# A two-layer hybrid encoder kernel: the second layer's output projection in seven block products, in one function with the gate

## What is computed

```python
# x: (1536, 1024), layer 1 (odd)
h = rmsnorm(x, g_pre)
z = h @ w_in                      # latents, gate g_c, FNet input f_in, gate g_d
c_out = mla_attention(...) * silu(g_c)        # 8 heads of 64 columns: 512 columns
d_out = fft2(f_in).real * silu(g_d)           # 512 columns
o = concat([c_out, d_out]) @ w_out            # output projection, 1024 x 1024
x = x + rmsnorm(o, g_post)                    # called x1 below
x = x + sigmoid(x @ w_ple_gate) * (p @ w_ple) # gate, 1024 x 1024, and embedding, 256 x 1024
```

## Time and profile before

| what | value |
|---|---|
| median of 3 runs | 1996.87 us (1994.7 to 2001.17) |
| the profiled execution | 1996.65 us, of which the span is 1994.9 |
| PE busy | 1921.7 us (96%), 9784 matmuls and transposes |
| DVE busy | 1143.9 us (57%) |
| ACT busy | 687.1 us (34%) |
| POOL busy | 761.8 us (38%) |
| DMA, share of 16 engines | 43.0% |
| mean granted PE clock | 0.987 of full speed |

### The profile page before, as it was taken

How to read it: one execution, slowest core, us unless ns; L and a number is a source line. 1 busy time by engine, 2 the same in 40 slices (tenths; PEclk the granted TensorE clock), 3 DMA queues, 4 the chain that set the end, 5 groups by cost and what they waited for, 6 DMA issues and landing times. The chain is left out here.

```text
span 1994.9 us, 26356 instructions
## 1 busy us (share of the span) xinstructions
PE 1921.7 (96%) x9784; PEld 1603.8 (80%) x9784; DVE 1143.9 (57%) x1735; ACT 687.1 (34%) x1409; POOL 761.8 (38%) x538
## 2 busy tenths in 40 slices
PE   4999999999989999999989999999999999999999
PEld 3888888887889788788877888877898998788787
DVE  5599999826768317524754100175777776234775
ACT  6111212211578332212223111122677775323322
POOL 0111121122587544454533222133699851531101
PEclk8999999999999999999989999999999999999999
DMA  4202333443476556534320222286546332656734
GB/s 171 64 11 69 133 95 109 144 141 114 164 260 219 182 165 223 198 114 135 131 66 15 79 90 69 88 326 182 165 133 201 121 105 64 229 209 225 259 126 145
DMA packets 152242, 286.11 MB, mean 143 GB/s; under 512 B 31489, under 2 KB 70145, under 8 KB 152130
## 3 DMA queue, kind: packets, MB, share of 16 engines
q1 hardware_dynamic: 152130, 284.62, 43.0%
HBM read 181.61 MB, written 102.96 MB: 143 GB/s over the span
## 5 line engine op out<-in xcount | busy, mean ns | idle before, releaser
L593 DVE SCALAR_TENSOR_TENSOR ie_acc<-ie_u,ie_wconv,ie_acc 128x1551 f32<-128x1551 f32 x120 | 249.8, 2081 | 3.2
L191 POOL TENSOR_TENSOR w_lo_part<-w_raw,w_hi_part 128x1024 fp32r<-128x1024 f32 x24 | 66.3, 2763 | 335.0 <-ACT w_hi_part L183 335.0
L1598 PE MATMUL op_ps<-w_hi_part,rows_hi 128*128 128x512 f32 x384 | 157.1, 409 | 5.0 <-DVE rows_lo L1157 2.6
L173 POOL TENSOR_TENSOR w_hi_part<-w_raw,zero 128x1024 fp32r<-128x1024 f32 x48 | 92.8, 1933 | 173.7 <-DMA w_raw<-wall 171.9
L328 PE MATMUL ie_ps<-rows_hi,w_hi_part 128*128 128x512 f32 x384 | 153.1, 399 | 4.8 <-DVE w_lo_part L557 4.8
L1598 PE MATMUL op_ps<-w_hi_part,rows_lo 128*128 128x512 f32 x384 | 152.3, 397 | 0.0
L328 PE MATMUL ie_ps<-rows_hi,w_lo_part 128*128 128x512 f32 x384 | 152.1, 396 | 0.0
L1598 PE MATMUL op_ps<-w_lo_part,rows_hi 128*128 128x512 f32 x384 | 152.1, 396 | 0.0
L328 PE MATMUL ie_ps<-rows_lo,w_hi_part 128*128 128x512 f32 x384 | 151.1, 394 | 0.0
L2870 DVE TENSOR_TENSOR mla_pt_lo<-mla_ps_t,mla_pt_hi 128x512 fp32r<-128x512 f32 x160 | 108.9, 686 | 26.2 <-ACT mla_pt_hi L2839 25.1
L175 POOL TENSOR_TENSOR w_lo_part<-w_raw,w_hi_part 128x1024 fp32r<-128x1024 f32 x48 | 119.1, 2480 | 3.8
(11 more groups left out here) (291 smaller groups left out, 5088.6 us busy)
## 6 DMA issues: line engine op xcount, KB each, us to landing
w_raw<-wall SPq DMA_DIRECT2D x76, 512.0 KB, 4.6
op_in<-x SPq DMA_DIRECT2D x24, 512.0 KB, 4.5
x<-op_in SPq DMA_DIRECT2D x24, 512.0 KB, 3.0
weight_blocks<-w_hi_part SPq DMA_DIRECT2D x20, 512.0 KB, 4.9
w_hi_part<-weight_blocks SPq DMA_DIRECT2D x14, 512.0 KB, 6.8
w_lo_part<-weight_blocks SPq DMA_DIRECT2D x14, 512.0 KB, 6.7
pro_x<-x SPq DMA_DIRECT2D x12, 512.0 KB, 7.9
op_in<-attn SPq DMA_DIRECT2D x24, 256.0 KB, 3.1
```

Of the source, the lines that this page charges most:

```text
L173: pool.tensor_tensor(hi, raw, g.zero[:, 0:1].broadcast_to([P, QCOLS]), ALU.add).then_inc(g.w_hi, 1)
L593: dve.scalar_tensor_tensor(acc[:], ubuf[:, cc, s:s + CW], wconv[:, cc, s:s + 1], acc[:], ALU.mult, ALU.add).then_inc(taps, 1)
L1598: mm = pe.matmul(product_at(c * NT + t), g.XT[a][:, k, t * P:(t + 1) * P], w_at(g, name, m, k * HALF, HALF), start=k + a + m == 0, stop=k ...
```

## The change

The gate's block scheme is used for the output projection too, and both run in one function, `out_and_gate`, over 84 units: 42 for the projection and 42 for the gate, each a product of 12 matmuls.

- `out_proj` is no longer called for layer 1, nor `gate_blocks`; the attention output stays in SBUF (`g.attn_rows`) and the half products too (`u`, `v`, `o11` in place of `o_half` in DRAM).
- The weights of both are summed, split and stored in blocks: 28 pieces in place of 14. 7 pieces each follow prep of heads 2, 3, 5 and 6; the sums of the gate's blocks (8 additions) follow prep of head 4. Their raw blocks are loaded by SP after the 14 pieces of the projection are stored.
- The high part of a piece is now made by ACT inside its attention stream (`wb.high`, after the exponential of steps 12h-2 to 12h+4), POOL makes the low part alone (`wb.low`). `wb.high` of piece p waits until the high part of piece p-2 is stored and its low part is made. ACT's attention stream is written out in place of the loop.
- The ring of split rows is 6 long and filled 5 ahead. The first 5 are filled in the last steps of the attention.
- x1 of a tile is made at the units of `X1_STEP`, by four DVE operations of 512 columns, and PE turns it right after the next unit.

```diff
 def mla(g, ml, bl, wb):
...
-        CHUNKS = {2: range(4), 3: range(4, 8), 4: range(8, 11), 5: range(11, 14)}
+        CHUNKS = {2: range(7), 3: range(7, 14), 5: range(14, 21), 6: range(21, 28)}
+        W_HIGH = {NT * h - 2 + i: p for h, c in CHUNKS.items() for i, p in enumerate(c)}
...
         def _(sp):
...
-            wb.load_raw(sp)
+            wb.load_raw(sp, 0)
             for h in range(2, HEADS):
                 sp.wait_ge(ml.prepped, h * ml.PREPS)
                 ml.load(g, sp, h, slice(h * DH, (h + 1) * DH))
-                for i in CHUNKS.get(h - 1, []):
-                    wb.store(sp, i)
-                if h % 2:
-                    pl.wait(sp, "normed", (h - 1) * NG)
-                    store(slice((h - 3) * DH, (h - 1) * DH))
+                for p in CHUNKS.get(h - 1, []):
+                    wb.store(sp, p)
+                if h == 4:
+                    wb.load_raw(sp, 1)
             wb.wait_stored(sp)
...
         def _(pool):
             for h in range(1, HEADS):
                 pl.wait(pool, "weighed", (h - 1) * NG)
                 ml.prep(g, pool, h, h % 2)
-                if h == 1:
-                    wb.sum(pool)
-                for i in CHUNKS.get(h, []):
-                    wb.split(pool, i)
-            for n in quarters("out1_a"):
-                split_quarter(g, pool, n)
+                if h in (1, 4):
+                    wb.sum(pool, h // 4)
+                for p in CHUNKS.get(h, []):
+                    wb.low(pool, p)
...
+            for step in range(LAST + DRAIN):
+                if 0 <= step - 2 < LAST:
+                    hi(0, step - 2)
+                if step % 2 and 0 <= step - 5 < LAST:
+                    act_copy(act, 0, (step - 5) // 2)
+                if step < LAST:
+                    exp(0, step)
+                if step in W_HIGH:
+                    wb.high(act, W_HIGH[step])
+                if step == LAST + 4:
+                    act.wait_ge(ml.prepped, HEADS * ml.PREPS)
+                    for N in range(AHEAD):
+                        bl.high(act, N)
...
+    def high(self, act, p):
+        m, b, q, name = self.piece(p)
+        act.wait_ge(self.summed, 8 * (m + 1))
+        if p >= 2:
+            act.wait_ge(self.hi_stored[p % 2], 16 * (p // 2))
+            act.wait_ge(self.lo, p - 1)
+        act.copy(self.stage(p), self.area(name, q)).then_inc(self.hi, 1)
+
+    def low(self, pool, p):
+        m, b, q, name = self.piece(p)
+        pool.wait_ge(self.hi, p + 1)
+        pool.tensor_tensor(self.area(name, q, True), self.area(name, q), self.stage(p).bitcast(F32), ALU.subtract).then_inc(self.lo, 1)
...
+RING, AHEAD = 6, 5
+X1_STEP = [33, 34, 36, 37, 39, 40, 42, 43, 44, 45, 46, 47]
...
+def out_and_gate(g, bl, wb):
...
+            def x1_row(t):
...
+                dve.scalar_tensor_tensor(left, left, r, wide(bl.gpost[:, 0:HALF]), ALU.mult, ALU.mult).then_inc(x1_rows, 1)
+                dve.scalar_tensor_tensor(right, right, r, wide(bl.gpost[:, HALF:D]), ALU.mult, ALU.mult).then_inc(x1_rows, 1)
...
+                dve.tensor_tensor(wide(x[:, 0:HALF]), wide(x[:, 0:HALF]), left, ALU.add).then_inc(x1_rows, 1)
...
+                dve.tensor_tensor(wide(x[:, HALF:D]), wide(x[:, HALF:D]), right, ALU.add).then_inc(x1_rows, 1)
...
+            for N in range(N_ALL):
+                product(N)
+                if 0 <= N - 4 < NT:
+                    turn_main(N - 4)
+                if N - 1 in x1_at:
+                    turn_x1(x1_at[N - 1])
+                if N in of_unit:
+                    embedding(of_unit[N])
...
-            rows = OutRows(g, 1)
-            mla(g, ml, rows)
-            ple = Ple(g, 1)
-            out_proj(g, 1, rows, ple)
-            gate_blocks(g, ple)
+            bl, wb = Blocks(g), WeightBlocks(g)
+            mla(g, ml, bl, wb)
+            out_and_gate(g, bl, wb)
```

891 lines of the change are left out of this document (507 added, 384 removed).

## The result

| what | before | changed kernel |
|---|---|---|
| median, first comparison | 1999.02 us (1994.7 to 2001.76, 4 runs) | 2017.85 us (2011.88 to 2020.67, 4 runs) |
| ratio to before, 95% interval | 1 | 1.0092 (1.0059 to 1.0125) |
| the profiled execution | 1996.65 us, span 1994.9 | 2011.88 us, span 2010.1 |
| attention, first to last score | 279.7 us | 306.9 us |
| last score to the end of the span | 319.7 us | 313.2 us |

The kernel became slower by 18.8 us in the medians. In the two profiled executions the difference is 15.2 us, but there the part ahead of the change, whose code is the same, was by chance 5.6 us shorter in the changed kernel (first score at 1389.94 against 1395.54). From the first score on it is +27.3 in the attention and -6.5 behind it, 20.8 us together.

The account below looks back on a forecast made before the run. It took PE to bound the kernel, with POOL next; terms -16.8 - 1.4 + 0.9 + 18.0 + 2.4 + 3.4 + 4 + 2.4 + 1 = +13.9 on 1996.65 us gave 2010.5 us, range 1982 to 2021.

Parts of the forecast that it names:

- Fewer matmuls, -16.8: Projection: 504 matmuls in place of 576, 72 fewer at 0.2332 us each, worth -16.8 us.
- The seam, -1.4: Attention to projection: first unit needs one DVE operation of 512 columns, not two of 1024; -1.4 us (0 to -2.65).
- Heads with a late store, 6.0 each: Attention heads 3, 5, 6: ACT waits for a store issued after prep and three loads; 6.0 us each, +18.0.
- Rival 1: Attention: stores are not held behind the loads and land within 5.5 us of head start; whole 1992.5 us, chance 0.17.
- Prep late, +0.9: Attention heads 3, 4 and 7: prep ends with nothing to spare, PE waits 0.3 us at each; +0.9 us.
- Clock, +4: Attention: PE's clock drops after three idle stretches near 5 us and one of 3.4, 1.0 each; +4 us (0 to 6.5).
- The gate's sums, +3.4: Attention, head 5: POOL's sums wait for raw blocks, making prep late, so PE waits 3.4 us (0 to 6.5).
- x1 in the middle, +2.4: Units 33 to 40: PE waits 0.4 us for DVE's x1, six times; +2.4 us (0 to 4).
- x loop, +1: From unit 42: three places for x rows form a loop with transfers at some 390 GB/s; +1 us (0 to 8).
- rival 3: Middle bound by DMA: x rows for tiles 8 to 11 land 2 us late each; whole 2018 to 2024, chance 0.12.
- The step that failed: Projection and gate: DVE's at most four operations of 0.7 us in the remaining units stay hidden; no waits counted.
- Rival 2: Attention: ACT has room for the casts, PE keeps 35.1 us a head; whole 1980 us, chance 0.14.

Follow-up runs that it names:

- e1: Changed kernel, with SP issuing the stores of a group's first two high parts before it waits for prep and issues the loads: 2021.45 us, ratio 1.0120.
- e6: Changed kernel, with all three loads of each head from the second on moving a twelfth of their bytes: 1994.26 us, ratio 0.9991.
- e12: Changed kernel, with only the values load of each head from the second on cut to a twelfth of its bytes: 2006.44 us, ratio 1.0049.
- e13: Changed kernel, with only the queries and keys loads from the second head on cut to a twelfth of their bytes: 1997.44 us, ratio 1.0015.
- e3: Changed kernel, with DVE collecting a gate unit's product ahead of the row sums and rows of the unit before: 2014.88 us, ratio 1.0097.
- e8: Changed kernel, with DVE collecting gate products first and SP loading embedding rows one output earlier: 2009.09 us, ratio 1.0065.
- e10: Changed kernel plus four staging places, earlier casts (spaced at head 2), early stores at head 5 only, raw blocks in halves, two gate edits: 1984.86 us, ratio 0.9937.
- e5: Changed kernel without ACT's 28 casts and POOL's 28 low parts, their sums, stores and loads kept: 1983.62 us, ratio 0.9936.

## Why the prediction was right, and where it was not

The forecast was 2010.5 us, slower by 13.9; the medians say 18.8, inside the range and on the side that had 0.64. Point by point:

- *Fewer matmuls, -16.8: right.* The projection's stretch fell from 151.2 to 129.6 us, 21.6 less, of which about 5.3 are six turns of x1 that lie now in the gate's units (0.88 each).
- *The seam, -1.4: right.* From last score to first product 8.7 in place of 10.3 us, the wait 0.98 in place of 2.65.
- *Heads with a late store, 6.0 each: right in place and cause, 1.0 too much in each.* The store landed 9.8 us into the head as forecast, ACT waited 5.7, 5.7 and 5.6 us against 5.7, and PE stood 5.1, 5.0 and 4.9. The step "is stored only after it saw prep end and issued three loads" is borne out by e1, where the store ahead of the loads lands in 3.4 us. What the forecast did not have is why the loads hold it: they do so by their bytes (e6, e12, e13), which a row of one late store could not tell from order alone. Rival 1, that the store "isn't held behind the loads", is refuted: it was, in every head. Before, the same transfers at the start of heads 2 and 3 were as dense (share 1.06 and 0.98, in the rows below) and the store as late, but POOL made both parts of a piece in turn, 4.3 us a piece, and nothing of the attention queued behind its wait. The change put the wait on an engine that had PE behind it.

```profile
1466.50:1476.50 10.00, 10.00 (x65) 8.76 (x65) 7.27 (x13) 7.07 (x15) 8.51 (x5) 1.00 1.06 325
1501.60:1511.60 10.00, 10.00 (x65) 8.72 (x65) 7.18 (x13) 7.20 (x15) 8.31 (x4) 1.00 0.98 321
```

- The rule of the Trainium skill, "DMA: Bandwidth & Descriptors", HWDGE ordering, that completion is not FIFO per issuing engine, did not help the store here: in the changed kernel and in e1 every transfer landed in its turn. Out of turn were only two small loads in e6 and one in e13, at most 0.9 us ahead of the raw blocks issued before them. The estimate worked out beside it, 3.2 us for a piece, goes by a figure that the page's section on the anatomy of one DMA has for transfers issued by GpSimd and that holds for one alone; here SP issues them, one alone took 2.6 us, and four under way together took 8.4 to 9.8 each. The same page, "Why small descriptors are slow", gives 27% overhead for runs of 256 bytes; e12 and e13 show one and a half times the time per byte.
- *Prep late, +0.9:* nothing at heads 3, 4 and 7; PE's one wait for POOL in the heads is that of head 5.
- *Clock, +4: too small, and by luck the attention came out near.* For the same instructions PE stood 17.7 us longer in the attention (20.9 against 3.1) and was busy 9.5 us longer (286.05 against 276.51), 8.6 of it in heads 3, 5 and 6. The forecast had 24.7 of waits and 4 of clock. The two errors nearly cancel: 27.3 against 28.7.

```profile
1395.54:1675.19 279.65, 276.51 (x1902) 248.81 (x1900) 215.90 (x346) 196.26 (x392) 204.69 (x86) 0.99 0.41 130
1389.94:1696.87 306.93, 286.05 (x1901) 255.28 (x1900) 216.77 (x346) 220.46 (x420) 213.48 (x86) 0.97 0.58 200
```

- *The gate's sums, +3.4:* POOL waited 2.7 for the raw blocks (3.7 forecast), PE 2.0.
- *x1 in the middle, +2.4:* 3.6. *x loop, +1:* nothing of its own; DVE waited 4.3 us for x in four waits, which PE sees only within those 3.6. The time is near the 2018 of rival 3, but its mechanism did not come, and the transfers ran at 295 GB/s from 1835 to 1870, not at 390.
- *The step that failed* is "DVE in the rest of the units has at most four operations of 0.7", and with it the claim that the ring's cover of 14 us hides them. It counts DVE's work, 4.1 us in a unit of 4.2, and not the loop through ACT, whose rounds took 5.6 to 5.7 us and once 7.5 where PE needs 4.18. That came out as 4.0 + 2.1 of waiting and 2.8 of slow clock, 8.9 us that no term had. Nor was the ring the cover that mattered: the wait is not one for `bl_ring`, as the forecast would have it, but for one of the 4 places of products. e3 and e8 took 5.9 and 8.9 us off the last part, to 304.3. The sum on record had 319.7 - 16.8 - 1.4 + 2.4 + 1 = 304.9 there.
- *Why 13.9 and not 18.8 or 20.8:* +8.9 for that loop, less 1.4 in the attention and 0.6 elsewhere. The places and causes of the attention's waits were forecast; that the middle of the forecast was only 5 us off owes something to errors against each other. Rival 2, that the attention hides all of it, needed more places for the stores to land in; e10, with the gate mended too, comes to 1984.9 where rival 2 said 1980.

## What to carry to other kernels

A wait for a store costs nothing on an engine with slack and nearly its full length on one that another engine depends on every 3 us: before work moves there, count the bytes that are issued ahead of each store and give it enough buffers for that landing time, since issuing one store sooner only shifts the wait to the next. For an engine that looks 95% full, follow one round of the loop through its partner engine, too; the round, not the sum of its operations, is its pace. And a group of transfers goes best where the transfer engines stand still, not where the code happens to be ready for it.

## What the runs showed of the hardware

- Transfers issued by SP landed in the order of their issue (the changed kernel and e1, from the first score on). Stores of 512 KB behind a head's loads took 8.4 to 9.8 us (changed kernel, head 3), one issued 0.37 us ahead of the loads 3.4 (e1), one alone 2.6.
- With 1607 short packets of 2057 the mean rate was 264 GB/s at a DMA share of 0.95 (changed kernel); with 62 of 565 it was 415 at 1.02 (e5, 1510 to 1515).
- A full DMA share for a whole head (0.94, 350 GB/s) slowed neither PE nor DVE nor ACT (e5).
- PE's granted clock fell to half, 1.2 GHz, behind idle stretches of 2.3 us (e3), 4.0 and 5.1 us; the wait of 4.0 us cost 6.8 in all, that of 5.1 in head 3 cost 8.3.
- Beside two operations of POOL on 128x1024 (1899.14 to 1904.2) two DVE operations with both inputs in SBUF took 2.38 and 2.12 us in place of 0.69, while a third in between, with one input in PSUM, took 0.67.
- The part ahead of the first score, the same code in all kernels, took from 1388.8 to 1397.6 us in their profiles, so differences of a few us are read from stretches, not from spans.
